# First two query/key/value chunks projected block by block, q/k norm weights folded into the rope tables, GpSimd out of the q/k norm

## What is computed

```
mod  = silu(c) @ w_mod + b_mod                    # shift1, scale1, ... from a (1024 x 6144) matrix
h    = layer_norm_plain(x) * (1 + scale1) + shift1
z    = h @ w_in                                   # 1024 -> 512 q + 128 k + 128 v + 512 xr + 512 gr
q    = rms_norm(q, q_g)  per head of 64           # x * rsqrt(mean(x^2) + eps) * g
k    = rms_norm(k, k_g)
q, k = axial_rope(q), axial_rope(k)               # latent tokens only
```

## Time and profile before

| | |
|---|---|
| time, median of 3 runs | 1002.07 us (1001.11 to 1003.17) |
| profiled execution: its time, its span | 1002.45 us, 1000.6 us |
| PE busy | 896.1 us (90%) |
| DVE busy | 773.8 us (77%) |
| ACT busy | 568.3 us (57%) |
| POOL busy | 192.1 us (19%) |
| mean TensorE clock granted | 0.958 of full speed |

### The profile page before, as it was taken

The page is one execution under the profiler, slowest core; times in us unless marked ns, Lnnn a source line. Parts: engine busy times, 40 slices in busy tenths (PEclk is TensorE's granted clock), DMA queues, the critical chain, the costliest instruction groups (busy, mean ns, idle before and its releaser), DMA issues.

```text
span 1000.6 us, 11569 instructions
## 1 busy us (share of the span) xinstructions
PE 896.1 (90%) x4616; PEld 608.3 (61%) x4616; DVE 773.8 (77%) x766; ACT 568.3 (57%) x568; POOL 192.1 (19%) x119
## 2 busy tenths in 40 slices
PE   4699899878779994589999999999999999999983
PEld 1388896345557882356666666666666666666651
DVE  3757540668874988578998999889999989998857
ACT  1525115854453223267777777777777777777742
POOL 1011402100234104200320331133023203310210
PEclk9899999989889997699999999999999999999997
DMA  8910400733004929699999999999999999999625
GB/s 325 383 50 10 186 1 21 266 104 118 1 1 169 356 85 401 240 369 369 350 414 377 380 383 403 378 378 394 398 380 374 407 386 376 382 410 387 229 55 181
DMA packets 57389, 272.08 MB, mean 272 GB/s; under 512 B 7028, under 2 KB 7272, under 8 KB 40952
## 3 DMA queue, kind: packets, MB, share of 16 engines
...
## 4 chain that ended last, share of the span: by engine, by line
PE 77%; DVE 9%; DMA 6%; ACT 4%; issue 4%; SPq 0%; POOL 0%; ACTq 0%; POOLq 0%; DVEq 0%
PE PS L839 22%; PE PS L841 22%; PE PS L840 22%; PE PS L984 2%; DMA ring<-in_w_mod 2%; PE PS L965 1%; DMA acc_scratch<-ysc,idx_u 1%; DVE WAl L1243 1%; DMA w_qkv<-in_w_in 1%; PE PS L952 1%; PE PS L1121 1%; PE PS L1132 1%; DMA xf<-acc_scratch 1%; PE PS L854 1%; PE PS L1006 1%
## 5 line engine op out<-in xcount | busy, mean ns | idle before, releaser
L1557 DVE TENSOR_TENSOR Wl<-wr,Wh 128x2048 fp32r<-128x2048 f32 x190 | 432.6, 2290 | 55.6 <-ACT Wh L759 54.5
L759 ACT ACTIVATE Wh<-wr 128x2048 fp32r<-128x2048 f32 x192 | 367.3, 1914 | 72.8 <-PE PS L841 72.7
L839 PE MATMUL PS<-Wh,Xh 128*80 128x512 f32 x512 | 203.6, 398 | 4.0 <-issue 2.9
L841 PE MATMUL PS<-Wl,Xh 128*80 128x512 f32 x512 | 202.4, 395 | 0.0
L840 PE MATMUL PS<-Wh,Xl 128*80 128x512 f32 x512 | 202.1, 395 | 0.0
L517 POOL DMA_INDIRECT acc_scratch<-ysc,idx_u x16 | 81.1, 5066 | 432.9 <-DVE ysc L1587 432.9
L839 PE MATMUL PS<-Wh,HTh 128*80 128x512 f32 x256 | 102.3, 400 | 3.1 <-DVE ysc L1587 3.1
L839 PEld LDWEIGHTS PS<-Wh,Xh 128*80 128x80 f32 x512 | 76.4, 149 | 44.6 <-issue 4.4
L841 PEld LDWEIGHTS PS<-Wl,Xh 128*80 128x80 f32 x512 | 76.2, 149 | 42.6 <-issue 0.9
L840 PE MATMUL PS<-Wh,HTl 128*80 128x512 f32 x256 | 100.9, 394 | 0.0
L841 PE MATMUL PS<-Wl,HTh 128*80 128x512 f32 x256 | 100.9, 394 | 0.0
...
## 6 DMA issues: line engine op xcount, KB each, us to landing
wr<-in_w_gate_up SPq DMA_DIRECT2D x128, 1024.0 KB, 8.2
...
w_qkv<-in_w_in SPq DMA_DIRECT2D x4, 768.0 KB, 11.9
...
```

Of the source, the lines that this page charges most:

```text
L759: act.activation(Wh[n % NWH][:], wr[s][:], ACT.Copy).then_inc(W_hi, 1)
L839: pe.matmul(out, w[0], x[0], start=first, stop=False)
L841: return pe.matmul(out, w[0], x[1], start=False, stop=last)
L1557: dve.tensor_tensor(Wl[s][:], wr[s][:], Wh[n % NWH][:].bitcast(F32), ALU.subtract).then_inc(W_lo, 1)
```

## The change

It has three parts.

- **k by k.** PE no longer transposes all eight blocks of h first. It runs the transposes of blocks 0 and 1, then for each k the transposes of block k + 2 and the k-th slice of chunks 0 and 1 together (`qkv(c, k)`). Chunks 2 to 4 are projected as before. To feed this, the first modulation row is transposed in the middle of the second group, ACT copies the second row before it splits any weights and then alternates one weight block with one h block, and DVE alternates `split_lo_w(k)`, `Hh(k)`, `Hl(k)`.
- **Norm weights in the rope tables.** DVE builds `gtab` (norm weight times cos and norm weight times sin, 16 small products) before the modulation columns. In the chain q and k are multiplied out of PSUM with both tables (`qc`, `qs`, `by_row`), one subtraction and one addition give the turned values, and the deviation is applied last to 640 columns. The prompt chunk, which has no rope, is multiplied with the norm weights alone. `gqk` is loaded on POOL's queue at the start instead of on SP's queue behind `w_qkv`.
- **POOL out.** The root is taken by ACT (`Sqrt`, whose table is loaded early by a dummy activation) and inverted by DVE (`reciprocal`, 128x10). The chain of chunk 4 is split: its sum and its products stand behind five of the eight ring splits, the rest behind the last three.

```diff
@@ SP, POOL
-                sp.dma_start(gqk[:, 0, :], t["q_norm_g"][0].partition_broadcast(P)).then_inc(misc_in, 16)
-                sp.dma_start(gqk[:, 1, :], t["k_norm_g"][0].partition_broadcast(P)).then_inc(misc_in, 16)
+        pool.dma_start(gqk[:, 0, :], t["q_norm_g"][0].partition_broadcast(P)).then_inc(cache_in, 16)
+        pool.dma_start(gqk[:, 1, :], t["k_norm_g"][0].partition_broadcast(P)).then_inc(cache_in, 16)
-        for c in range(CH):
-            pool.wait_ge(ss_ok, c + 1)
-            pow_mhalf(rsq[:, c % 2, :], ssq[:, c % 2, :], 10, 1.0 / HD).then_inc(rs_ok, 1)
@@ ACT
+        act.activation(table_scr[:], epsc[:], ACT.Sqrt)
...
-            for k in range(4 * g, 4 * g + 4):
-                act.wait_ge(w_qkv_in[k // 2], 16)
-                split_w(k, w_qkv, QKV)
-        act.wait_ge(modT_ok, 2)
         for k in range(KC):
+            act.wait_ge(w_qkv_in[k // 2], 16)
+            split_w(k, w_qkv, QKV)
+            if k == 0:
+                act.wait_ge(modT_ok, 2)
             act.wait_ge(h_t, k + 1)
...
+            act.wait_ge(ss_ok, c + 1)
+            act.activation(rsq[:, c % 2, :], ssq[:, c % 2, :], ACT.Sqrt, bias=epsc[:, 0:1], scale=1.0 / HD).then_inc(rs_ok, 1)
@@ PE
+        pe.wait_ge(ct_ok, 2)
+        mod_group(0, 0)
+        mod_group(1, 4, range(0, 4))
+        pe.wait_ge(mrow_ok, 1)
+        row_transposes(m_rowA[0], 1)
+        mod_group(1, 4, range(4, 8))
+        pe.wait_ge(xn_ok, CH)
+        h_transposes(0)
+        pe.wait_ge(mrow_ok, 2)
+        row_transposes(m_rowA[1], 3)
+        h_transposes(1)
...
+        for k in range(KC):
+            if k + 2 < KC:
+                h_transposes(k + 2)
+            pe.wait_ge(h_lo, k + 1)
+            pe.wait_ge(split_lo, k + 1)
+            for c in range(2):
+                last = qkv(c, k)
+                if k == KC - 1:
+                    last.then_inc(q_ps, 1)
+        for c in range(2, CH):
+            pe.wait_ge(q_free, c - 1)
+            pe.wait_ge(v_ok, c - 1)
@@ DVE
+        for g in range(2):
+            for w in range(2):
+                for c in range(PC):
+                    dve.tensor_tensor(gtab[:, g, w, c, :].rearrange("p (a b n) -> p a b n", a=2, b=2),
+                                      gqk[:, g, :].rearrange("p (a b n) -> p a b n", a=2, b=2),
+                                      rope[:, c, w, :].rearrange("p (a n) -> p a n", a=2).unsqueeze(2).broadcast_to([P, 2, 2, 16]),
+                                      ALU.mult)
+        mod_cols(0, 1, 0, 0.0)
+        mod_cols(1, 3, 1, 1.0)
+        for k in range(KC):
             split_lo_w(k, w_qkv, QKV)
...
+        def qk_rows(c):
+            dve.wait_ge(sq_ok, c + 1)
+            dve.wait_ge(v_ok, c + 1)
+            dve.tensor_reduce(ssq[:, c % 2, :], heads(sq[:], 10), AX.X, ALU.add).then_inc(ss_ok, 1)
+            if c < PC:
+                by_row(qc, b, gtab[:, 0, 0, c, :], gtab[:, 1, 0, c, :])
+                by_row(qs, b, gtab[:, 0, 1, c, :], gtab[:, 1, 1, c, :]).then_inc(q_free, 1)
+            else:
+                by_row(qc, b, gqk[:, 0, :], gqk[:, 1, :]).then_inc(q_free, 1)
+        def qk_finish(c):
...
+                dve.tensor_tensor(pairs(y[:])[:, :, :, 0, :], x1c, x2s, ALU.subtract)
+                dve.tensor_tensor(pairs(y[:])[:, :, :, 1, :], x2c, x1s, ALU.add)
+            dve.wait_ge(rs_ok, c + 1)
+            link(dve.reciprocal(rsq[:, c % 2, :], rsq[:, c % 2, :]))
+            link(dve.tensor_tensor(heads(y[:], 10), heads(src[:], 10), rsq[:, c % 2, :].unsqueeze(2).broadcast_to([P, 10, HD]),
+                                   ALU.mult))
...
+        for c in range(PC):
+            qk_rows(c)
+            qk_finish(c)
+        for n in range(8, 13):
+            split_lo_w(n, ring, 1024)
+        qk_rows(PC)
+        for n in range(13, 16):
+            split_lo_w(n, ring, 1024)
+        qk_finish(PC)
```

More of the change, by code:

```diff
@@ L861, in row_transposes, with h_transposes @@
             last.then_inc(mrow_t, 1)
-        pe.wait_ge(ct_ok, 2)
-        mod_group(0, 0)
-        mod_group(1, 4)
-        for g in range(2):
-            pe.wait_ge(mrow_ok, g + 1)
-            row_transposes(m_rowA[g], 4 + g)
-        pe.wait_ge(xn_ok, CH)
-        pe.wait_ge(modT_ok, 2)
-        for k in range(KC):
+        def h_transposes(k):
             if k >= 2:
@@ L1072, in _ @@
         pe.wait_ge(rg_ok, RJ)
-        pe.wait_ge(misc_in, 48)
+        pe.wait_ge(misc_in, 16)
         for n, k in enumerate(K_OUT):
@@ L1244, in split_lo_w @@
                               ALU.subtract).then_inc(split_lo, 1)
-        for k in range(4):
-            split_lo_w(k, w_qkv, QKV)
-        mod_cols(0, 4, 0, 0.0)
-        mod_cols(1, 5, 1, 1.0)
-        for k in range(4, KC):
-            split_lo_w(k, w_qkv, QKV)
-        for k in range(KC):
+        dve.wait_ge(cache_in, 80)
+        for g in range(2):
[8 more added lines that the diff above has]
+        for k in range(KC):
+            split_lo_w(k, w_qkv, QKV)
             dve.wait_ge(hmod_ok, k + 1)
@@ L1268, in pairs, with by_row @@
             return ap.rearrange("p (h a b n) -> p h a b n", h=10, a=2, b=2)
-        for c in range(CH):
+        def by_row(dst, b, q_row, k_row):
+            dve.tensor_tensor(heads(dst[:, 0:QW], 8), heads(bank(b), 8), q_row.unsqueeze(1).broadcast_to([P, 8, HD]), ALU.mult)
+            return dve.tensor_tensor(heads(dst[:, QW:640], 2), heads(bank(b + 1, 0, KVW), 2),
+                                     k_row.unsqueeze(1).broadcast_to([P, 2, HD]), ALU.mult)
+        def qk_rows(c):
             b = 2 * (c % 2)
@@ L1282, in _ @@
-            last.then_inc(q_free, 1)
+            if c < PC:
[4 more added lines that the diff above has]
+        def qk_finish(c):
+            y = qr[c % 2]
             dve.wait_ge(q_free, c + 1)
-            dst = qn if c < PC else qr[c % 2]
             if c >= 2:
                 dve.wait_ge(qk_t, c - 1)
-            dve.tensor_tensor(heads(dst[:, 0:QW], 8), heads(qn[:, 0:QW], 8),
-                              gqk[:, 0, :].unsqueeze(1).broadcast_to([P, 8, HD]), ALU.mult)
@@ L1304, in _ @@
-            dve.tensor_copy(kd[c % 2][:].rearrange("p (g h d) -> p g h d", g=2, h=2),
-                            heads(qr[c % 2][:, QW:640], 2).unsqueeze(2).broadcast_to([P, 2, 2, HD])).then_inc(qr_ok, 1)
-            if c == CH - 2:
-                for n in range(8, 16):
-                    split_lo_w(n, ring, 1024)
+                x1c, x2c = pairs(qc[:])[:, :, :, 0, :], pairs(qc[:])[:, :, :, 1, :]
+                x1s, x2s = pairs(qs[:])[:, :, :, 0, :], pairs(qs[:])[:, :, :, 1, :]
+                dve.tensor_tensor(pairs(y[:])[:, :, :, 0, :], x1c, x2s, ALU.subtract)
@@ L1590, in one_hot @@
         def one_hot():
-            dve.wait_ge(misc_in, 64)
+            dve.wait_ge(misc_in, 32)
             dve.wait_ge(x_t, 2 * NE)
```

56 lines of the change are left out of this document (15 added, 41 removed).

## The result

| | before | after |
|---|---|---|
| median of 4 runs each, on one chip | 1002.62 us (1001.11 to 1003.34) | 993.82 us (991.39 to 994.71) |
| profiled execution: time, span | 1002.45 us, 1000.6 us | 993.92 us, 992.1 us |

A forecast was written before the change was run, and what follows sets the result against it. TensorE's 90% busy share decided little; between 26 and 117 us it read PE's gaps and the waits filling them. Terms -8.6 + 0.3 + 2.8 - 3.4 = -8.9 took the median of 1002.07 to 993.2 us, range 990.8 to 997.3.

The forecast's parts named there:

- step 1: Front, modulation's end to k loop's end: projection starts earlier and PE sets the pace of the k loop, -8.6 us.
- step 2: Start of the kernel: the two broadcast loads moved to POOL's queue ahead of the w_mod stream cost +0.3 us, at most 1.0.
- step 3: Ahead of chunk 2: PE newly waits for the banks of chunk 0, +2.8 us.
- step 4: Tail, end of chunk 3 to j = 1: POOL's root and two DVE operations per latent chain leave, -3.4 us.
- One of its signs: After the k loop: the squares of chunks 0 and 1 start about 1.05 us apart, as a sign of being right.
- The rival on the clock: Behind the new gap ahead of chunk 2: the clock falls to 1.2 GHz, +3.3 us, 996.5 us; chance 0.17.
- main case: Whole kernel: the sum of the four steps, 993.2 us, own range 991.2 to 995.0; chance 0.62.
- the clock at half behind 63: PE's clock after the new wait ahead of chunk 2: half rate behind 63 us would show the prediction wrong.

The follow-up runs named there:

- e9: e2 plus two loads of 32 KB on POOL's queue at the start, each 128 different rows of 256 B, read by nothing: 990.36 us.
- e10: e2 plus the two broadcasts of the one 256 B row, issued by ACT at its start, read by nothing: 993.11 us.
- e1: The kernel before with only the two gqk broadcast loads moved to POOL's queue at the start: 1004.44 us, ratio 1.0027.
- e2: The changed kernel with the gqk loads back on SP's queue and the table products behind the k loop: 990.44 us, ratio 0.9889.
- e7: e2 with the chain of chunk 4 behind all eight ring splits instead of five: 990.98 us, ratio 0.9903.
- e12: The kernel of e2 once more, unchanged, on another chip: 995.38 us, profiled.
- e3: The kernel before with the k by k part alone; chain, POOL and loads as before: 999.59 us, ratio 0.997.
- e11: e2 plus one broadcast of the one row instead of two, on POOL's queue, read by nothing: 990.68 us.
- e4: e2 with the front of before (h transposes first, chunk after chunk), so chain and tail alone: 997.01 us, ratio 0.9957.
- e5: e2 with chunk 1 three slices behind chunk 0 at the k loop's end and the products out of PSUM ahead of the sum: 988.88 us, ratio 0.9881.
- e6: e2 with nine matmuls into an unread bank issued ahead of the wait before chunk 2: 989.04 us, ratio 0.9886.
- e8: e2 with the edits of e5 and e7 together: 987.84 us, ratio 0.9869.

## Why the prediction was right, and where it was not

The time was right within 0.6 us, and part of that is luck. The mechanism of steps 1, 3 and 4 was right. But at j = 1, where all terms of the sum meet, the trace shows 6.2 us and not 8.9: the broadcasts and the fall of the clock took 3.7 us more than forecast, steps 1 and 4 gave 1.0 more. Another 2.3 us behind j = 1, for which the prediction has no term, made up the difference.

| term | forecast | in the trace of the changed kernel |
|---|---|---|
| step 1, from the modulation's end to the end of the k loop | -8.6 | -8.9 |
| step 2, the broadcasts | +0.3 | +2.7 |
| step 3, the wait ahead of chunk 2 | +2.8 | +2.8 |
| the clock behind it (a rival) | 0 | +1.3 |
| step 4, the tail | -3.4 | -4.1 |
| sum at j = 1 | -8.9 | -6.2 |
| behind j = 1 | 0 | -2.3 |

**Step 1 was right in mechanism and size.** Modulation end to first projection matmul 4.23, forecast 4.25. One k costs 2.64 us on PE (its groups of five transposes start at 45.17 and 47.81), forecast 2.7; PE sets the pace. The loop's last matmul has drained at 65.25 - 2.50 = 62.75. Less a drain of 0.28 and counted from the modulation's end that is 23.75 us, where it was 68.72 - 36.05 = 32.67: -8.9. The table products took 2.25 us in all, 0.14 each, and were hidden.

**Step 2 failed, by 2.4 us.** It priced the loads by their bytes and by a stretch in which small pieces of other loads ran, with 1.0 as the upper end. The row of that stretch was also misread. Its share of 0.50 says that the DMA engines were idle for half of that microsecond, not that small pieces run at half rate: 177 GB/s at 0.50 are 354 per full share, against 367/0.97 = 378 from 36 to 52. So it does not bear out a rule on small pieces. In the changed kernel 25 GB/s went with a share of 1.29. For separate rows the price of 0.3 is not exceeded (e9: 0.12). The repeated row costs 2.7 and no row of before showed it from POOL's queue; the same loads stood behind `w_qkv` on SP's, where nobody waited for them. The Trainium skill (DMA: Bandwidth & Descriptors, Specifications), on which the prediction drew for pieces under 512 B, does not tell e9 from the broadcasts, and the measurement decides. The same page (Issuing engine by pattern) says that the queues of SP and ACT are generally faster than GpSimd's. e10's 0.75 against 2.8 points the same way but doesn't show it, since its loads were also issued 2.6 us earlier.

**Step 3 was right:** the wait from the drained array to the first matmul was 2.50 us, which is the forecast's 2.8 less the 0.28 of a drain. From chunk 0's squares to PE's start it took 65.25 - 61.75 = 3.50, forecast 0.94 + 0.82 + 1.75 = 3.51. One of its signs failed without harm: the squares of chunks 0 and 1 start 2.10 apart (61.75 and 63.85) and not 1.05, since on ACT the root of chunk 0, which waits for DVE's sum, now stands between them.

**The rival on the clock came true beside the main case.** Squares of chunk 0 to squares of chunk 2 took 75.25 - 61.75 = 13.50 us, and 12.24 in e9 (71.32 - 59.08), so the fall cost 1.3; forecast 3.3 from a longer stretch at half clock. The forecast also named "the clock at half behind 63" as a sign of being wrong, and in this it was. The weighing was at fault too: one trace with a wait of 2.18 and no fall was taken as evidence against. e1 shows a fall behind 2.19. At the two places in question, ahead of chunk 2 and of j = 1, waits of 2.2 to 2.5 us on PE went with a fall in six traces (after, e1, e2, e7, e10, e12) and with none in four (before and e3 at j = 1, e9, e11). Where PE had no such wait ahead of chunk 2 (before, e1, e4, e5, e6, e8), the clock didn't fall there in any of the six traces. That ties the fall to the wait; what decides it from one execution to the next stays open. In the attention stage a wait of 2.65 us went with a fall in all 14 traces, in the changed kernel here:

```profile
245.49 1.18 PE L990 MATMUL PS<-consts,prob 128*128 128x128 f32 x5 [2.65 <-DVE PT L556]
```

```profile
246.00:247.00 1.00, 1.00 (x8) 0.67 (x8) 0.38 (x2) 0.30 (x1) 0.00 (x0) 0.50 0.00 0
```

So the prediction's main case and this rival were not two cases of the kernel, but two outcomes of one execution. The Trainium skill (TensorE: Matmul & The Clock Gate, HAM oscillation) counts the cost of a throttled stretch as half its length. From 65.25 to 69 the clock misses 0.75 x 0.50 + 0.50 + 0.50 + 0.07 = 1.4 us of full speed, by the rows shown for 65 to 69; the squares say 1.3. The trace agrees.

**Step 4 was right in mechanism and 0.7 us too small.** Counted from the end of chunk 3 (84.10), the ring splits on ACT start at 3.04 (forecast 3.2) and end at 10.7 (11.6), since a split takes 7.69/8 = 0.96 there against 1.05 in the earlier trace rows. Eight times this difference is the 0.7. The 1.05 was probably no cost of ACT's own: each of these splits waits until PE has used up the block it overwrites, and PE needs 1.05 us for one block of chunk 4. Where ACT starts them 1.97 us behind the end of chunk 3 (before, e1, e3) they take 8.41 us in all, where it starts at 3.04 or later (after, e2, e4 to e8) 7.69 or 7.70. DVE has done its five splits at 11.6 (11.9) and does not wait for ACT; its sum and products end at 13.3 (14.1) and its last splits at 16.7 (17.5: 97.28 + 3.48 on its timeline). j = 1 starts at 18.3 (19.0).

**Behind j = 1 it was luck, as far as the runs can tell.** The two programs are the same there. From the marker to the first matmul of the output projection it is:

| trace | before | after | e1 | e2 | e3 | e4 | e5 | e6 | e7 | e8 | e9 | e10 | e11 | e12 |
|---|---|---|---|---|---|---|---|---|---|---|---|---|---|---|
| us | 195.43 | 193.92 | 194.05 | 195.88 | 195.36 | 195.63 | 194.03 | 193.78 | 196.09 | 195.38 | 195.45 | 194.31 | 194.08 | 195.55 |

The stretch of before and that of after, same work, with the same waits in them:

```profile
200.00:311.45 111.45, 86.81 (x731) 58.15 (x729) 83.36 (x124) 59.18 (x115) 25.08 (x18) 0.89 0.15 51
```

```profile
193.75:303.70 109.95, 85.07 (x730) 56.77 (x728) 83.52 (x124) 59.28 (x115) 24.95 (x18) 0.89 0.15 51
```

PE is busy for 1.74 us less with one instruction less in the records, at the same DVE and ACT. The front of before (before, e1, e4) and that of the change lie on both sides of the table, as do e9 and e11, which differ only in a load at the start. So I read 1.5 of the 2.3 us as the scatter of that stage and not as the change. The other 0.8 lie behind it, where the gather `Xg` landed 0.9 us sooner (5.98 against 6.89); whether that is chance I did not test.

Between traces and medians something stays open. The marker moved by 6.25 us, and the interval of the ratio is 6.8 to 11.1. For e1 to e8 the two stand like this:

| | e1 | e2 | e3 | e4 | e5 | e6 | e7 | e8 |
|---|---|---|---|---|---|---|---|---|
| marker against 115.95, us | +4.2 | -8.75 | -2.5 | -4.4 | -11.4 | -10.1 | -9.4 | -12.9 |
| ratio x 1002, us | +2.7 | -11.1 | -3.0 | -4.3 | -11.9 | -11.4 | -9.7 | -13.1 |

They agree within 0.5 us except in e1, e2 and e6. The trace of before had no fall behind its wait at j = 1 and that of e1 had one, at the price of about 1.5 (4.17 of the marker less the 2.65 of the modulation); an execution of before that has it makes the change look better by that much. This is an argument from two traces, not a count.
